# First mix of a fused block: queries and keys of a head group projected together by token tile, the queries' inverse root moved into the masking step, and a new order on VectorE

## The reference, cut to what matters

```python
h = rms_norm(x, norm1_g[l])
proj = h @ w_in[l]                       # 1024 -> 3*512 + 2*512
q, k, v, u = jnp.split(proj, [ATTN_WIDTH, 2 * ATTN_WIDTH, 3 * ATTN_WIDTH], axis=-1)
q = apply_rope(rms_norm(q, q_norm_g[l]), cos, sin)      # 8 heads of 64
k = apply_rope(rms_norm(k, k_norm_g[l]), cos, sin)
attn = moba_attention(q, k, v)           # at 256 tokens: causal softmax attention, scale 1/8
conv = conformer_conv(u, glu_b[l], dw_w[l], dw_b[l], conv_ln_g[l], conv_ln_b[l])  # 31 taps
x = x + jnp.concatenate([attn, conv], axis=-1) @ w_out[l]
```

## Time and profile before

| what | us |
|---|---|
| median of three runs | 1323.35 |
| the profiled execution | 1324.39 |
| its span, first to last instruction | 1322.6 |
| PE busy | 1306.3 |
| DVE busy | 828.0 |
| ACT busy | 682.9 |
| POOL busy | 136.7 |

### The profile page before, as it was taken

One profiled execution on the slowest core, in us unless ns is written; L12 is line 12 of the kernel. 1 busy time (PEld: TensorE's weight loads), 2 busy tenths in 40 slices (PEclk: granted clock), 3 DMA queues, 4 the chain that ended last, 5 costly groups with the idle time before them and its releaser, 6 DMA issues.

```text
span 1322.6 us, 18723 instructions
## 1 busy us (share of the span) xinstructions
PE 1306.3 (99%) x7310; PEld 1134.6 (86%) x7310; DVE 828.0 (63%) x992; ACT 682.9 (52%) x912; POOL 136.7 (10%) x162
## 2 busy tenths in 40 slices
PE   8999999999999999999999999999999999999998
PEld 7988888888888887888888888888888998888886
DVE  6997755565655558777765556665565545665553
ACT  6776544453544445556554445444454665554441
POOL 2770000000000001112100000000001441000000
PEclk9999999999999999999999999999999999999999
DMA  8334775553755545326575554675553744465540
GB/s 280 128 112 144 242 251 191 190 192 112 254 206 189 186 122 160 96 96 217 186 233 190 190 191 139 212 254 190 190 191 135 236 127 132 160 209 190 191 156 32
DMA packets 174352, 234.98 MB, mean 178 GB/s; under 512 B 4351, under 2 KB 154127, under 8 KB 174288
## 3 DMA queue, kind: packets, MB, share of 16 engines
q1 hardware_dynamic: 170368, 223.52, 50.7%
q0 software_dynamic: 3184, 9.37, 2.3%
q10 hardware_dynamic: 736, 1.19, 0.2%
HBM read 233.03 MB, written 1.05 MB: 177 GB/s over the span
## 4 chain that ended last, share of the span: by engine, by line
PE 92%; DVE 5%; DMA 2%; ACT 1%; issue 1%; POOL 0%; SPq 0%; DVEq 0%; ACTq 0%
PE psum L1156 22%; PE psum L1078 15%; PE psum L1080 15%; PE psum L1079 15%; PE psum L1160 12%; DVE w_lo L1719 2%; PE psum L1121 2%; PE psum L1120 2%; PE psum L1119 2%; PE psum L1350 1%; DMA raw<-in_w_in 1%; PE psum L1358 1%; PE psum L1248 1%; PE psum L1349 1%; PE psum L1367 1%; PE psum L1368 1%
## 5 line engine op out<-in xcount | busy, mean ns | idle before, releaser
L1719 DVE TENSOR_TENSOR w_lo<-raw,w_hi 128x2048 fp32r<-128x2048 f32 (+1 forms) x209 | 480.8, 2306 | 91.7 <-ACT w_hi L456 90.5
L456 ACT ACTIVATE w_hi<-raw 128x2048 fp32r<-128x2048 f32 (+1 forms) x212 | 402.6, 1905 | 40.6 <-PE psum L1080 11.2
L1156 PE MATMUL psum<-t_both,w_hi 128*128 128x512 f32 x1280 | 327.5, 393 | 0.0
L1156 PEld LDWEIGHTS psum<-t_both,w_hi 128*128 128x128 f32 x1280 | 230.2, 189 | 41.0
L1078 PE MATMUL psum<-w_hi,f_hi 128*128 128x512 f32 x488 | 192.8, 395 | 0.0
L1080 PE MATMUL psum<-w_hi,f_lo 128*128 128x512 f32 x488 | 190.2, 390 | 0.0
L1079 PE MATMUL psum<-w_lo,f_hi 128*128 128x512 f32 x488 | 190.1, 389 | 0.0
L1160 PEld LDWEIGHTS psum<-t_both,w_lo 128*128 128x128 f32 x1280 | 174.6, 190 | 12.3
L1160 PE MATMUL psum<-t_both,w_lo 128*128 128x256 f32 x1280 | 178.5, 282 | 0.0
L1078 PE MATMUL psum<-w_hi,t_both 128*128 128x512 f32 (+2 forms) x464 | 167.4, 361 | 2.8 <-DVE g_row L1959 2.7
L1080 PE MATMUL psum<-w_hi,t_both 128*128 128x512 f32 (+2 forms) x464 | 163.1, 351 | 0.0
(11 more groups left out here) (190 smaller groups left out, 1473.8 us busy)
## 6 DMA issues: line engine op xcount, KB each, us to landing
raw<-in_ffn_wg SPq DMA_DIRECT2D x44, 1024.0 KB, 5.5
raw<-in_ffn_wu SPq DMA_DIRECT2D x44, 1024.0 KB, 5.2
raw<-in_ffn_wd SPq DMA_DIRECT2D x44, 1024.0 KB, 5.0
raw<-in_even_w_in SPq DMA_DIRECT2D x12, 1024.0 KB, 5.1
raw<-in_odd_w_in SPq DMA_DIRECT2D x12, 1024.0 KB, 5.3
raw<-in_w_gate SPq DMA_DIRECT2D x11, 1024.0 KB, 5.5
raw<-in_w_up SPq DMA_DIRECT2D x11, 1024.0 KB, 5.3
raw<-in_w_down SPq DMA_DIRECT2D x11, 1024.0 KB, 4.9
```

What stands on the lines that cost most here:

```text
L456: nc.scalar.activation(w_hi[:, n % SLOTS, 0:w], raw[:, n % RAWS, 0:w], ACT.Copy).then_inc(hi_done, 1)
L1156: mm = nc.tensor.matmul(o[:, :], wh[:, k, cs], t_both[:, k, :, :].rearrange("p a s -> p (a s)"), start=k == 0, stop=k == KT - 1)
L1719: nc.vector.tensor_tensor(w_lo[:, n % SLOTS, 0:w], raw[:, n % RAWS, 0:w], w_hi[:, n % SLOTS, 0:w].bitcast(F32), ALU.subtract).then_inc(lo_ ...
```

## The change

Six things, all in the first mix.

1. The units are reordered: queries 0 to 3 (4), keys 0 to 3 (5), values (6), queries 4 to 7 (7), keys 4 to 7 (8), values (9). Units 4 and 5, and 7 and 8, are made as pairs: for each token tile one group of 24 matmuls that stream 512 columns, 256 of queries and 256 of keys (`pair_tile`). A tile's first 12 matmuls need only high parts, then come four more, and the last eight need the low parts.
2. What was "a unit of queries" or "of keys" for both token tiles is now one token tile of both.
3. The queries are not multiplied by their inverse root any more. It stays in `st` and enters as the per-row factor of masking (`row_scale`). The 1/8 and a minus sign go into the queries' rotary table, and the causal mask changes sign. `rope_end` becomes three instructions of 256 elements in place of two of 512: add for keys, add for queries, multiply for keys.
4. The order on DVE is new (see below).
5. On ACT and POOL the taps, squares and roots stand in other places.
6. PE turns unit 7 after step 10, where unit 6 was turned after step 8.

```diff
+                    tile_rows = lambda t: qk[:, :, 2 * i:2 * i + 2, t * P:(t + 1) * P].rearrange("p u c s -> p c u s")
+                    return [(w, HW * t + UC * i, UC, ("rope", 64, tile_rows(t), t)) for t in range(T)]
...
-                ph["units"] = glu(0) + glu(1) + [keys(0), queries(0), keys(1), val(0), queries(1), val(1)]
+                ph["units"] = glu(0) + glu(1) + turned(0) + val(0) + turned(1) + val(1)
                 ph["bank"] = [0, 1] * 5
+                ph["pairs"] = [4, 7]
...
                     root(0)
                     add(3)
                     root(1)
-                    add(3)
+                    add(6)
                     root(2)
-                    add(7)
+                    add(4)
                     root(3)
...
+                def pair_tile(u, t, part):
+
+                    n, b = n0 + u, ph["bank"][u + t]
+                    o, ts = bank[b][:, :], slice(t * P, (t + 1) * P)
+                    if part == 0:
+                        pe.wait_ge(bank_free[b], left[u + t] - 1)
+                        pe.wait_ge(hi_done, n + 2)
+                    for k in (range(6), range(6, KT))[part]:
+                        nc.tensor.matmul(o, t_hi[:, k, ts], pair_cols(w_hi, n, k), start=k == 0, stop=False)
+                        nc.tensor.matmul(o, t_lo[:, k, ts], pair_cols(w_hi, n, k), start=False, stop=False)
+                    if part:
+                        pe.wait_ge(lo_done, n + 2)
+                        for k in range(KT):
+                            mm = nc.tensor.matmul(o, t_hi[:, k, ts], pair_cols(w_lo, n, k), start=False, stop=k == KT - 1)
+                        mm.then_inc(*((unit_used, 2) if t else (pair_half, 1)))
...
-                turned_after = {4: 4, 6: 5, 8: 6, 11: 8}
+                turned_after = {4: 4, 6: 5, 10: 7, 11: 8}
...
                     ins = nc.vector.tensor_tensor_reduce(
-                        out=s_buf[:, h % 2, lo:hi], in0=bank[4][:, lo:hi], in1=L["mask"](h, t), scale=-L["scale"],
+                        out=s_buf[:, h % 2, lo:hi], in0=bank[4][:, lo:hi], in1=L["mask"](h, t),
+                        scale=L["row_scale"](h, t) if "row_scale" in L else -L["scale"],
...
                 def rope_end(j):
                     r, c_, s_, dst = parts[j]
-                    link(nc.vector.tensor_tensor(c_, c_, s_, ALU.add))
-                    dve.wait_ge(rstd_ready, nx(rstd_ready))
                     if r >= 2:
                         dve.wait_ge(rope_T, r - 1)
...
+                    keys = step(nc.vector.tensor_tensor(c_[:, 1, :, :], c_[:, 1, :, :], s_[:, 1, :, :], ALU.add))
+                    nc.vector.tensor_tensor(dst[:, 0, :, :], c_[:, 0, :, :], s_[:, 0, :, :], ALU.add)
+                    dve.wait_ge(dve_step, keys)
+                    dve.wait_ge(rstd_ready, nx(rstd_ready))
+                    per = st[:, root_at(r) + 4:root_at(r) + 8].unsqueeze(2).broadcast_to([P, 4, 64])
+                    nc.vector.tensor_tensor(dst[:, 1, :, :], c_[:, 1, :, :], per, ALU.mult).then_inc(roped, 1)
...
-                taps(7)
+                taps(5)
                 split_to(6)
                 glu(3)
-                taps(5)
+                taps(3)
                 split_to(7)
```

More of the change, by code:

```diff
@@ L53, in host_tables @@
     zero = np.zeros((P, P), np.float32)
-    causal = np.where(k <= q, 0.0, NEG).astype(np.float32)
+    causal = np.where(k <= q, 0.0, -NEG).astype(np.float32)
     chunky = np.where(k // 64 <= q // 64, 0.0, NEG).astype(np.float32)
@@ L133, in attention_plan, with root_at @@
                         nmax=st[:, 80:80 + 2 * heads], sum=st[:, 112:112 + 2 * heads])
+        def root_at(r):
+            return (32, 40, 48, 64)[r]
         def wide4(h):
@@ L690, in mix_first @@
                 gate(2)
-                taps(2)
                 split_to(6)
-                taps(2)
+                taps(4)
                 split_to(7)
                 taps(3)
+                square(4)
                 split_to(8)
-                square(4)
                 taps(2)
@@ L704, in mix_first @@
                 split_to(10)
-                square(6)
+                keep_unit(ph, 6)
                 taps(2)
@@ L709, in mix_first @@
                 split_to(11)
-                keep_unit(ph, 7)
+                square(7)
                 exps(L, 0)
@@ L714, in mix_first @@
                 taps(2)
-                keep_rope(units[6][3], 7)
                 keep_pt(L, 0)
@@ L721, in mix_first @@
                 exps(L, 2)
-                taps(3)
+                taps(2)
+                keep_rope(units[7][3], 7)
+                taps(1)
                 keep_pt(L, 2)
@@ L1592, in mix_first @@
                 lo0 = seen[id(t_lo_ok)]
+                def pair_tile(u, t, part):
[12 more added lines that the diff above has]
+                        mm.then_inc(*((unit_used, 2) if t else (pair_half, 1)))
                 def tile(u, t):
                     b = ph["bank"][u]
+                    first = [v for v in (u, u - 1) if v in ph["pairs"]]
+                    if first:
+                        pair_tile(first[0], u - first[0], t)
+                        return
                     if t == 0:
@@ L2066, in mix_first @@
                 rope_begin(5)
-                taps(2)
                 rope_end(5)
+                split_to(9)
+                split_to(10)
+                taps(1)
+                maxima(L, 0)
                 mean_square(2)
-                rope_begin(6)
-                split_to(9)
-                maxima(L, 0)
-                rope_end(6)
-                taps(5)
+                rope_begin(7)
                 maxima(L, 1)
-                split_to(10)
+                rope_end(7)
                 taps(3)
                 maxima(L, 2)
-                taps(2)
                 mean_square(3)
@@ L2084, in mix_first @@
                 rope_end(8)
-                split_to(11)
-                taps(4)
+                taps(6)
                 maxima(L, 4)
@@ L2090, in mix_first @@
                 group_out(L, 0, V["o"][0], 6)
-                taps(2)
+                split_to(11)
                 maxima(L, 6)
                 group_lo(0, 6)
-                taps(4)
+                taps(6)
                 maxima(L, 7)
@@ L2317, in setup @@
                     g = qk_g[:, i, :].unsqueeze(1).broadcast_to([P, T, 64])
-                    nc.vector.tensor_tensor(qk_rope[:, i, :, 0:64], rope[:, :, 0:64], g, ALU.mult)
-                    nc.vector.tensor_tensor(qk_rope[:, i, :, 64:96], rope[:, :, 64:96], g[:, :, 32:64], ALU.mult)
-                    ins = nc.vector.tensor_tensor(qk_rope[:, i, :, 96:128], rope[:, :, 96:128], g[:, :, 0:32], ALU.mult)
+                    for to, at in ((slice(0, 64), slice(0, 64)), (slice(64, 96), slice(32, 64)), (slice(96, 128), slice(0, 32))):
+                        ins = nc.vector.scalar_tensor_tensor(out=qk_rope[:, i, :, to], in0=rope[:, :, to], scalar=(-0.125, 1.0)[i],
+                                                             in1=g[:, :, at], op0=ALU.mult, op1=ALU.mult)
                 ins.then_inc(setup_done, 1)
```

21 lines of the change are left out of this document (10 added, 11 removed).

## The result

| | before | after |
|---|---|---|
| median, us (8 executions each, same chip) | 1323.39 (1320.84 to 1324.0) | 1326.82 (1325.67 to 1327.84) |
| profiled execution | 1324.39 | 1325.67 |
| its span | 1322.6 | 1323.9 |

The ratio is 1.0034, with a 95% interval of 1.0025 to 1.0042. The changed kernel is slower by 3.4 us. The forecast was +1.0 and "no change that can be measured"; the time is inside the range given, near its upper end. The slowdown is small and still clear of the noise, and its direction was not forecast: "slower" had a chance of 0.23.

What follows compares the result with a forecast made beforehand. PE was taken as the bound, busy 1306.3 of 1322.6 us. 1324.39 - 5.1 (stalls, half clock, wider matmuls) + 0.4 (middle wait) + 4.1 (tail) + 1.6 (half clock) = 1325.4, so median about 1324.3; range 1321.5 to 1327.5.

Steps and rivals of the forecast that it cites:

- part 3: Tail of DVE's queue, first mix: 19 taps behind the last masking make PE wait 3.1 us; channel mean 4.1 late.
- four us of idleness: PE's idleness around the tail, over twice the earlier 1.81 us idle, so the half clock was expected again.
- The half clock behind the tail (1.6): After PE's tail wait the clock falls to 1.2 GHz: 1.4 to 1.7 us lost, 1.6 taken.
- the clock does not fall: Rival: no half clock follows the tail's wait, giving 1322.8 us; chance 0.14.
- The half clock in the middle (1.5 of the 5.1): Half clock after PE's 1.8 us wait for unit 5's rotary step: losing it was to gain 1.5 us.
- taking off 1.04: Step from the profiled execution's forecast, 1325.4, to the median's, 1324.3: the profiled one is 1.04 us above the median.
- The other waits of the middle (0.4): PE's possible new wait for unit 8's low part: 0 to 1.3 us, taken as 0.4.
- part 2: Middle of the first mix: the 1.8 us wait goes; wrong if PE waits over 1.5 us between 53 and 62.
- The later roped units have over 1 us to spare: In the first mix, roped units after unit 8's low part come over 1 us before PE needs them.
- second rival: DVE meets POOL's additions at two rope_end steps; PE waits 2.4 us for unit 8's low part: 1327.8; chance 0.18.
- DVE's busy time did not fall by 2 to 4 us: Sign to look for in the profile after: DVE's busy time lower by 2 to 4 us.
- The wider matmuls (1.5, "all on the path"): Pairs' matmuls of 512 columns instead of 256 save PE 1.2 to 1.5 us, all on the path; 1.5 taken.

Runs made afterwards that it cites:

- a_best: One of the follow-up kernels; the text does not say which, nor its time. Its profile has mean clock 0.998 and a fall only behind the last matmul.

## Why the prediction was wrong

**The tail (part 3): right.** Wait 3.1 forecast, 3.12 measured, of 9.5 us of DVE's work forecast and 9.57 measured; the channel mean late by 4.1 forecast, 4.37 measured. The close 3.12 is in part luck: DVE came 0.9 us late to the last masking, inside the 0.2 to 1.2 of the working, and PE came 0.8 us late to the turn, through the wait for head 6's exponential that the working did not have. The first lengthens the wait at the turn, the second shortens it; without the second it would have been near 3.9. The working's "four us of idleness" is one wait of 3.12 and one of 0.77, 5 us apart. (Rows 9 put the end of the first quotient at 92.03 where the working has 91.95, which changes nothing.) The same taps alone cost the kernel before 4.7, and taking most of them out of the changed kernel gives 4.7 back.

**The half clock behind the tail (1.6): right for the median.** In the six kernels with the 3 us wait, 41 of 50 executions have a mean clock of 0.998 or less. Five of the six have executions of both sorts, and those at 0.999 are 1.2 to 1.8 us shorter than the rest, though there are only one to three of them in each. The rival "the clock does not fall" is what the profiled execution did.

**The half clock in the middle (1.5 of the 5.1): the step that failed.** The working took the 1.5 us from the profiled execution of before, where a fall did follow the wait of 1.8 us, and counted it as a gain; then it went from that execution to the median by taking off 1.04. But the fall is an event of some executions. Of 96 executions of before, 20 have a mean clock of 0.998, with a median of 1323.8; the 76 others have 0.999 or 1.0, with medians of 1323.1 and 1323.6. The profiled one has 0.998. The profile of the kernel with the tail's taps alone has the same middle with neither the wait of 1.8 nor the fall. So the median of before holds no fall, and there was nothing to regain. (The 20 are only 0.2 to 0.7 us longer than the others, less than the 1.5 of a fall. Some of them may have no fall among the matmuls, as the one of `a_best`; these runs do not show it.) Setting the sum against the profile's own time is sound, but taking off 1.04 and no more hid that the fall was already missing from the median. Starting from the median without it, the same sum gives 1323.35 - 3.6 + 0.4 + 4.1 + 1.6 = 1325.9.

**The other waits of the middle (0.4): too small by 1.1.** The low part of unit 8 came near the upper end of its bounds: in the changed kernel's profile its wait is 1.14, with 0.29 ahead of it (together 1.4, just under the 1.5 that was to tell part 2 wrong) and 0.35 behind. "The later roped units have over 1 us to spare" was wrong: PE waits 0.2 to 0.4 us for the last one in six of the twelve profiles of the changed kernel and its variants. The leg from unit 4 to the last scores is 57.2 us in the changed kernel's profile, and 56.3, 56.3, 56.5 and 56.0 with the taps forward, the square earlier, narrow matmuls and the constant; before without its fall is 59.97 - 1.5 = 58.5 (58.8 in the profile of the tail alone). So a typical execution gains about 2.1 there, not 3.2. The mechanism was the second rival's, meetings with POOL, at less than its price: five steps of DVE's chain were stretched by 4.2 us in all. The low part ended at 58.94, not after 60.0, and no second fall came. The rival's time of 1327.8 is nearer to the measured 1326.8 than the forecast's 1324.3, though the wait of 2.4 us that it names did not come. The bounds of the working allowed four meetings (4.4 us), the value taken some three. The same stretching is the likely reason why DVE's busy time did not fall by 2 to 4 us; with short additions of POOL it is 818.4 us in place of 828.4, but no run shows what short additions would do to the kernel before.

**The wider matmuls (1.5, "all on the path"): wrong place.** PE's busy time fell by 0.8 us between the same marks against the narrow ones, and no time followed, because DVE's chain set the pace.

**The corrected sum.** 1323.35 - 2.1 (middle) + 4.3 (tail) + 1.4 (half clock behind it, most executions) = 1326.95, against 1326.82 measured. The miss of 2.5 us is 1.5 for the fall that the median never had and 1.1 for the waits of the middle. The sum closes this well only with the middle of four variants' profiles: with the 57.2 of the changed kernel's own profile the gain would be 1.3 and the sum 0.8 higher. So the 1.5 is surer than the 1.1, which one profile more or less moves by most of a microsecond.

**What stays open.** Why the fall follows one wait and not another. Why the executions of before at 0.998 are not longer by the whole price of a fall. And how much of the column's cost in masking reaches the end.

## What to carry to other kernels

Before a loss seen in the profiled execution is counted as a gain, see whether the median execution has it: the mean clock and the time of every other execution show it, if roughly. Work moved behind the last producer of a chain must be weighed against the consumer's own work over the same leg (here 9.5 against 6.4 us), whatever it frees ahead; it is the surest number in a reordering. Where two engines take turns, count each step of the critical chain that can meet the other engine, and take the upper half of the bounds when the other engine's work is dense; a faster bound engine (here wider matmuls) is worth nothing while such a chain sets the pace.

## What the runs showed of the hardware

- The half clock follows some waits and not others of the same length. It came with an idle of 1.42 us in one profile, of 1.81 in another, and of 2.95 to 3.14 in three; it did not come with 3.12 to 3.14 in three others, nor with 1.7 between 500 and 550 us, nor with 1.14 or less in the first mix. By the mean clocks, which tell it most of the time: 0.998 or less in 20 of 96 executions of before, in 41 of 50 with the 3 us wait, and in 5 of 66 of the six kernels whose profiles have no wait over 1.2 us in the first mix behind the start-up. Each fall among the matmuls lasted 3.41 us, and began between 0.5 us before and 0.9 us after the end of the idle time. One fall cost 1.48 us in the leg where two profiles can be compared.
- A meeting with a POOL addition lengthened a short and a long DVE step by the same 1.1 us: one of 0.41 to 1.52 and one of 2.28 to 3.37. POOL's own additions grow too, from 1.3 us to 3.14 beside low parts.
- A masking instruction (`tensor_tensor_reduce`) with its factor in a column takes 0.34 us for 128 columns and 0.47 for 256, against 0.28 and 0.41 with a constant: 0.06 us each.
- The waits of the table understate what short waits cost. The leg of the changed kernel is 2.7 us longer than with POOL's short additions, and its listed waits sum to 1.8; PE's busy time over the leg takes the other 0.8 (55.33 against 54.54).
